# Hybrid GLA and Mamba-2 layer: conditioning weights in two column halves, raw first turns, an own bank for the turn of k

## The reference

```python
shift, scale, gate = jnp.split(jax.nn.silu(c) @ ada_w + ada_b, 3, axis=-1)
h    = rms_norm(x, pre_norm_w) * (1.0 + scale) + shift
proj = h @ w_in                       # q, k, v, g, gate code, z, xBC, dt
# GLA group, 4 heads, keys of 128, values of 256:
log_a = jax.nn.log_sigmoid(code @ gla_gate_w2 + gla_gate_b) / 16
o = rms_norm(gla_chunked(q, k, v, log_a), gla_norm_w) * jax.nn.silu(g)
# SSD group, 16 heads of 64: causal conv + SiLU on xBC, chunked scan, gated group norm -> y
mixed = jnp.concatenate([o, y], axis=-1) @ w_out
x = x + gate * rms_norm(mixed, post_norm_w)
```

## Time and profile before

| | |
|---|---|
| Time, median of 3 runs | 1843.85 us (1842.21 to 1844.53) |
| Profiled execution: its time | 1843.53 us |
| Profiled execution: its span | 1841.8 us |
| TensorE busy | 1692.6 us (92%), 9620 matmuls |
| VectorE, ScalarE, GpSimd busy | 879.9 (48%), 813.8 (44%), 241.6 us (13%) |
| DMA | 172.20 MB, mean 93 GB/s |
| Mean granted TensorE clock | 0.973 |

### The profile page before, as it was taken

How to read it: one execution, slowest core, us unless ns; L and a number is a source line. 1 busy time by engine, 2 the same in 40 slices (tenths; PEclk the granted TensorE clock), 3 DMA queues, 4 the chain that set the end, 5 groups by cost and what they waited for, 6 DMA issues and landing times. The chain is left out here.

```text
span 1841.8 us, 26172 instructions
## 1 busy us (share of the span) xinstructions
PE 1692.6 (92%) x9620; PEld 1456.8 (79%) x9620; DVE 879.9 (48%) x1593; ACT 813.8 (44%) x1412; POOL 241.6 (13%) x369
## 2 busy tenths in 40 slices
PE   2799989998999899988999999999999599999998
PEld 2578777777788778877889898888988477888886
DVE  5444443354343433345676668766676453222221
ACT  1565555545554555554445546545544441111110
POOL 5000000000000000000222121222222201000000
PEclk8799999999999999998999999999999899999999
DMA  8422151135122412224111134212210174222221
GB/s 255 144 87 104 50 169 58 53 113 156 62 62 72 119 61 67 80 58 126 64 64 63 63 109 144 75 64 68 91 57 34 58 239 150 91 91 91 91 91 46
DMA packets 102142, 172.20 MB, mean 93 GB/s; under 512 B 7459, under 2 KB 75315, under 8 KB 98086
## 3 DMA queue, kind: packets, MB, share of 16 engines
q1 hardware_dynamic: 98918, 154.05, 25.8%
q10 hardware_dynamic: 2304, 16.78, 2.4%
q0 software_dynamic: 832, 0.22, 0.1%
HBM read 137.21 MB, written 33.82 MB: 93 GB/s over the span
## 5 line engine op out<-in xcount | busy, mean ns | idle before, releaser
L960 PE MATMUL ps<-hl,w 128*128 128x512 f32 x1536 | 391.5, 405 | 0.0
L1841 PE MATMUL ps<-d_w,d_yh 128*128 128x512 f32 x1536 | 354.2, 393 | 16.6 <-DVE d_yh L1798 11.0
L1841 PEld LDWEIGHTS ps<-d_w,d_yh 128*128 128x128 f32 x1536 | 290.7, 190 | 80.0 <-DVE d_yh L1798 11.4
L960 PEld LDWEIGHTS ps<-hl,w 128*128 128x128 f32 x1536 | 288.4, 192 | 60.6 <-issue 0.9
L1577 PE MATMUL ps<-hl,w 128*128 128x256 f32 x2304 | 294.6, 288 | 5.1 <-POOL c_past L1266 5.1
L1577 PEld LDWEIGHTS ps<-hl,w 128*128 128x128 f32 x2304 | 282.5, 193 | 13.3 <-issue 7.7
L966 PE MATMUL ps<-w,hl 128*128 128x256 f32 x1536 | 201.1, 287 | 0.0
L966 PEld LDWEIGHTS ps<-w,hl 128*128 128x128 f32 x1536 | 191.3, 191 | 2.5
L1458 DVE SCALAR_TENSOR_TENSOR c_acc<-c_before,conv_col,c_acc 128x256 f32<-128x256 f32 x288 | 142.3, 494 | 79.8 <-ACT c_acc L1342 72.8
L1581 PE MATMUL ps<-hl 128*128 128x512 f32 x768 | 178.7, 392 | 0.0
L1581 PEld LDWEIGHTS ps<-hl 128*128 128x128 f32 x768 | 143.0, 188 | 29.4
(11 more groups left out here) (227 smaller groups left out, 2185.1 us busy)
## 6 DMA issues: line engine op xcount, KB each, us to landing
x_sb<-h SPq DMA_DIRECT2D x52, 512.0 KB, 3.9
c_ac<-step_sums ACTq DMA_DIRECT2D x16, 1024.0 KB, 4.7
w_raw<-in_w_in SPq DMA_DIRECT2D x30, 512.0 KB, 5.2
c_h_raw<-h SPq DMA_DIRECT2D x56, 256.0 KB, 2.8
d_y_raw<-mixed_in SPq DMA_DIRECT2D x7, 2048.0 KB, 8.6
ada<-in_ada_w SPq DMA_DIRECT2D x8, 1024.0 KB, 17.9
x_sb<-in_x SPq DMA_DIRECT2D x16, 512.0 KB, 6.7
mixed_in<-y SPq DMA_DIRECT2D x32, 256.0 KB, 2.5
```

The costliest lines, as they stand in the source:

```text
L960: mm = pe.matmul(ps[:, PROJ + u % 2, :], w[:, u, k, a, :], hl[:, par, k, b, :], start=(k == 0 and i == 0), stop=(k == KT - 1 and i == 2))
L1841: mm = pe.matmul(ps[:, 2 * t + j, :], yh[:, t, f, a, :], w[:, f, c, j * 512:(j + 1) * 512], start=(f == 0 and i == 0), stop=(f == FT - 1 a ...
```

## The change

Three things are changed, and the order of the first block's work follows from them.

- `ada` is held as two halves of the columns: shift and scale of columns 0 to 3 of tiles, then of 4 to 7. SP loads eight row blocks of the first half (0.5 MB each, pieces of 2 KB), block 0 of x, two weights, the eight row blocks of the second half, the third weight, block 1 of x. Each half is summed, multiplied into its own bank (`MODS`) and made into gains by itself.
- TensorE turns all of block 0 before it has any gain; ScalarE copies the raw turns to SBUF (`first_copy`), and scaling reads them there. Weights 0 and 1 are split next, and units 0 and 1 of step 0 are multiplied column by column beside the codes (`first_units`), columns 0 to 3 before, 4 to 7 after the second half's sum. Step 0 starts at slot 4. The squares and the norming of block 1 come before it, after the copies of units 0 and 1, of the code and the split of weight 3; the soft gate of step 0 moves from slots 2 and 3 to 4 and 5, `gate_sums` from 4 to 6, `exps` from 6 to 8, the splits of weights 4 and 5 to slots 5 and 7.
- The turn of k goes to bank `LEFT` in rounds 3, 5 and 7 to 14 (`k_turns`; round r is computed in step r+1), where it doesn't wait for y; the turn of o waits for y instead. In every step the table set with Exp and Ln is loaded right after Silu. In `ssd`, TensorE no longer waits for that block's constants at its start.

```diff
-    FIRST_TURNS = (2, 3, 4, 5, 7)
+    FIRST_TURNS = (2, 3, 4, 5)
+    MODS = (7, 5)
...
+        def k_turns(r):
+            return TURNS if r + 1 < NB or r + 1 in (SIZES_AT, GATE_AT + 1) else LEFT
...
-                def load_ada(k):
-                    sp.dma_start(ada[:, k, :], ada_w[0, k * P:(k + 1) * P, 0:2 * D]).then_inc(ada_loaded[k], 16)
+                def load_ada(j, r):
+                    wait(sp, ada_loaded[r], j * 16)
+                    src = ada_w[0, r * P:(r + 1) * P, 0:2 * D].rearrange("p (s n) -> p s n", s=2)
+                    sp.dma_start(ada[:, j, r, :].rearrange("p (s n) -> p s n", s=2), src[:, :, j * HK * P:(j + 1) * HK * P]
+                                 ).then_inc(ada_loaded[r], 16)
...
-                for k in range(KT):
-                    load_ada(k)
-                    if k == 1:
+                for r in range(KT):
+                    load_ada(0, r)
+                    if r == KT - 1:
                         load_x(0)
-                for u in range(AHEAD):
-                    load_w(0, u)
+                load_w(0, 0)
+                load_w(0, 1)
+                for r in range(KT):
+                    load_ada(1, r)
+                load_w(0, 2)
...
+                def first_copy(k):
+                    act.wait_ge(turned, k + 1)
+                    act.activation(first_full[:, k, :], ps[:, FIRST_TURNS[k % 4], :], ACT.Copy).then_inc(first_raw, 1)
...
                     act.activation(gz[:, n % 2], gz[:, n % 2], ACT.Silu).then_inc(gsilu, 1)
+                    act.preload_act_table_set("natural_log_exp_and_others")
...
+                    gate_at = 4 if n == 0 else 2
+                    for i in range(4 if n == 0 else 0, 3 * TB):
...
-                        if i == 2:
+                        if i == gate_at:
                             gate_in(n)
-                        if i == 3:
+                        if i == gate_at + 1:
                             soft_gate(n)
...
-                        if i % 2 == 1 and n == 0 and i // 2 + AHEAD < U:
-                            w_high(0, i // 2 + AHEAD)
+                        if n == 0 and i in (5, 7):
+                            w_high(0, (i - 5) // 2 + UV)
...
-                        if i == 6:
+                        if i == gate_at + 4:
...
-                act.wait_ge(gain_ready, 1)
+                for k in range(KT):
+                    first_copy(k)
+                w_high(0, 0)
+                w_high(0, 1)
                 for k in range(0, KT, 2):
-                    even_full(0, k, FIRST_TURNS[k % 5])
+                    act.wait_ge(gain_ready, k // HK + 1)
+                    if k == 0:
+                        act.wait_ge(first_raw, KT)
+                    even_full(0, k, first_full[:, k, :])
                     high(0, k)
                     high(0, k + 1)
-                    if k // 2 < AHEAD:
-                        w_high(0, k // 2)
+                    if k == HK - 2:
+                        w_high(0, 2)
+                code_part(0)
+                evacuate(0, 0)
+                evacuate(0, 1)
+                code_high(0)
+                w_high(0, 3)
+                for t in range(TB):
+                    x_square(1, t)
...
+                def add_ada(j, r):
+                    dve.wait_ge(ada_loaded[r], (j + 1) * 16)
+                    if r == 0:
+                        dve.tensor_scalar(ada_sum[:, j, :], ada[:, j, r, :], c_act[:, r:r + 1], None, ALU.mult
+                                          ).then_inc(sum_ready, 1)
+                    else:
+                        dve.wait_ge(sum_ready, j * KT + r)
+                        dve.scalar_tensor_tensor(out=ada_sum[:, j, :], in0=ada[:, j, r, :], scalar=c_act[:, r:r + 1],
+                                                 in1=ada_sum[:, j, :], op0=ALU.mult, op1=ALU.add).then_inc(sum_ready, 1)
+
+                def gains(j):
+                    ks = slice(j * HK, (j + 1) * HK)
+                    dve.wait_ge(mod_done, j + 1)
+                    dve.tensor_copy(mod[:, :, ks], ps[:, MODS[j], 0:KT].rearrange("p (s k) -> p s k", s=2)).then_inc(mod_ready, 1)
+                    dve.wait_ge(mod_ready, j + 1)
+                    dve.scalar_tensor_tensor(out=gain[:, ks], in0=mod[:, 1, ks], scalar=1.0, in1=pre_col[:, ks],
+                                             op0=ALU.add, op1=ALU.mult).then_inc(gain_ready, 1)
+                    dve.wait_ge(gain_ready, j + 1)
+
+                def first_pair(k):
+                    odd_full(0, k + 1, first_full[:, k + 1, :])
+                    low(0, k)
+                    low(0, k + 1)
+
                 dve.wait_ge(c_ready, 1)
-                for i, k in enumerate(BY_SUMS):
-                    dve.wait_ge(ada_loaded[k], 16)
-                    if i == 0:
-                        dve.tensor_scalar(ada_sum[:, :], ada[:, k, :], c_act[:, k:k + 1], None, ALU.mult).then_inc(sum_ready, 1)
-                    else:
-                        dve.wait_ge(sum_ready, i)
-                        dve.scalar_tensor_tensor(out=ada_sum[:, :], in0=ada[:, k, :], scalar=c_act[:, k:k + 1],
-                                                 in1=ada_sum[:, :], op0=ALU.mult, op1=ALU.add).then_inc(sum_ready, 1)
-                    if i == 1:
-                        x_normed(0)
+                for r in range(KT):
+                    add_ada(0, r)
                 dve.wait_ge(wg_hi, 1)
                 dve.tensor_tensor(wg[:, :, L0:L0 + RC], wg_raw[:, :, :], wg[:, :, 0:RC].bitcast(F32),
                                   ALU.subtract).then_inc(wg_ready, 1)
                 dve.wait_ge(w2_hi, 2)
                 dve.tensor_tensor(w2[L0:L0 + RANK, :], w2_raw[:, :], w2[0:RANK, :].bitcast(F32),
                                   ALU.subtract).then_inc(w2_ready, 1)
-                dve.wait_ge(mod_done, 1)
+                x_normed(0)
                 dve.wait_ge(cols_loaded, 32)
-                dve.tensor_copy(mod[:, :], ps[:, PROJ, 0:2 * KT]).then_inc(mod_ready, 1)
-                dve.wait_ge(mod_ready, 1)
-                dve.scalar_tensor_tensor(out=gain[:, :], in0=mod[:, KT:2 * KT], scalar=1.0, in1=pre_col[:, :],
-                                         op0=ALU.add, op1=ALU.mult).then_inc(gain_ready, 1)
-                dve.wait_ge(gain_ready, 1)
-                for k in range(0, KT, 2):
-                    odd_full(0, k + 1, FIRST_TURNS[(k + 1) % 5])
-                    low(0, k)
-                    low(0, k + 1)
-                    if k // 2 < AHEAD:
-                        w_low(0, k // 2)
+                gains(0)
+                dve.wait_ge(first_raw, KT)
+                first_pair(0)
+                w_low(0, 0)
+                w_low(0, 1)
+                for r in range(KT):
+                    add_ada(1, r)
+                    if r == 1:
+                        first_pair(2)
+                    if r == 3:
+                        w_low(0, 2)
+                gains(1)
+                first_pair(4)
+                first_pair(6)
+                code_sum(0)
+                code_low(0)
+                w_low(0, 3)
+                x_normed(1)
...
+                def mods(j):
+                    pe.wait_ge(sum_ready, (j + 1) * KT)
+                    bias = ada_col[:, :].rearrange("p (s k) -> p s k", s=2)[:, :, j * HK:(j + 1) * HK]
+                    pe.matmul(ps[:, MODS[j], 0:KT].rearrange("p (s k) -> p s k", s=2), ident[:, :], bias, start=True, stop=False)
+                    for f in range(KT):
+                        mm = pe.matmul(ps[:, MODS[j], f:f + 1], ada_sum[:, j, f * P:(f + 1) * P], ones[:, 0:1], start=False,
+                                       stop=(f == KT - 1))
+                    mm.then_inc(mod_done, 1)
+
+                def first_units(k):
+                    codes(0, k)
+                    for u in range(2):
+                        if k == 0:
+                            pe.wait_ge(w_ready, u + 1)
+                        for i, (a, b) in enumerate(PASSES):
+                            mm = pe.matmul(ps[:, PROJ + u, :], w[:, u, k, a, :], hl[:, 0, k, b, :],
+                                           start=(k == 0 and i == 0), stop=(k == KT - 1 and i == 2))
+                        if k == KT - 1:
+                            mm.then_inc(unit_done, 1)
...
                     wait(pe, kt_ready, m)
-                    wait(pe, y_ready, m)
+                    if k_turns(r) == TURNS:
+                        wait(pe, y_ready, m)
                     cols = slice(t * P, (t + 1) * P)
-                    pe.transpose(ps[:, TURNS, 0:DK], k_end[:, cols], ident[:, :]).then_inc(kt_done, 1)
+                    pe.transpose(ps[:, k_turns(r), 0:DK], k_end[:, cols], ident[:, :]).then_inc(kt_done, 1)
...
                     pe.wait_ge(kt_ready, m + 1)
+                    wait(pe, y_ready, m)
...
-                pe.matmul(ps[:, PROJ, 0:2 * KT], ident[:, :], ada_col[:, :], start=True, stop=False)
-                pe.wait_ge(c_ready, 1)
```

(49 more changed lines are left out.)

33 lines of the change are left out of this document (18 added, 15 removed).

## The result

| | before | after |
|---|---|---|
| time, median | 1843.03 us (1837.94 to 1844.53, 4 runs) | 1823.68 us (1822.90 to 1825.26, 4 runs) |
| ratio after/before, 95% interval | | 0.9901 (0.9880 to 0.9922) |
| profiled run / its span | 1843.53 / 1841.8 us | 1824.41 / 1822.7 us |
| ScalarE busy | 813.8 us | 783.7 us |
| granted clock, mean | 0.973 | 0.972 |

The account below looks back on a forecast made before the run. The prediction took TensorE's chain of waits, ending in an output projection fed without a break, as the bound. Terms of +8.3 and -27.0 net -18.7 us: a span of 1823.1, forecast 1825 us, range 1814 to 1838.

Parts of the forecast that it names:

- The opening: Up to the first turn of block 1: that turn at 87.2 us against 85.54, a loss of 1.7.
- Steps 0 to 2: Start of the gated attention: longer TensorE waits, +4.0 us in step 0 and +0.9 each in steps 1 and 2.
- the term of 0.8 for a low clock: In steps 0 to 2: longer gaps may buy one more low-clock stretch, +0.8 us (0 to 3).
- The table loads: Gated attention: three loads out, one in, per step; terms of -9.0, -6.3, -3.7, -1.5 and +1.8 us.
- The own bank: Gated attention: k's turn no longer waits for y in ten rounds; -5.1, -1.2 and -1.3 us.
- rival D: Table loads: the preload fails, Exp and Ln go on loading their own sets; 1843 us, no change; 6%.
- B: Opening: it gains after all, with x in by 19 and the clock high; 1816 us; 15%.
- C: Attention: waits are handed on to another input, so 27 saved becomes 14; 1838 us; 14%.
- E: Step 0 and three quarters of step 1: TensorE's clock stays low, costing 27 us more; 1852 us; 5%.
- The entry of the SSD part: Start of the SSD part: without the wait for constants TensorE starts at about 839.7, not 840.40; -0.7 us.

Follow-up runs that it names:

- e3_early_x: The changed kernel with the second block of x squared and normed ahead of the second half of the first units; 1812.12 us.
- e5_late_load: The changed kernel with the table load at the end of ScalarE's slot 7 instead of straight after Silu; 1813.22 us.
- e1_no_load: The changed kernel without the table load after Silu; 1831.87 us.
- e4_old_opening: The kernel before with the load, the bank and the entry of the SSD part changed, its opening left as it was; 1819.62 us.
- e8_bank_alone: The kernel before with the own bank for the turn of k as its only change; 1826.93 us.

## Why the prediction was right, point by point

**The opening** was worked out right in its order and nearly in its times. Last square at 23.76 (23.1 said), TensorE's turns from 31.40 (30.9), the second gain ready at 62.03 (63.1), block 1 at 86.52 (87.2). One size was off: the 32 turns took 5.56 us, 0.17 each, not 0.22. In the trace the first 18 start 0.21 us apart, the rate of the prediction, and the last 13 only 0.11. Half the distance looks like the clock's two levels, though the profile gives 1.00 for the whole stretch. The turns began 0.5 late and ended 1.1 early, and so the second half of the sums ended 1.2 early; the rest of the chain, a little longer than priced, left 0.7 of that. That block 1 waits because x is squared and normed behind the first units is shown by e3_early_x.

**Steps 0 to 2** cost 8.9 from block 1's turn to the start of step 3, where 6.6 was said. The waits are nearly those of the text: 2.87 at slot 6 of step 0 (3 said), 3.38 and 3.37 in steps 1 and 2 (3.4 said). At slot 8 of step 0 the 3.5 came in two pieces, 1.99 for the last weight, which the text had not named, and 1.37. What was too small is the term of 0.8 for a low clock: there were new stretches in steps 0, 2 and 3, and one in step 7 in place of another; only that of step 5 went.

**The table loads.** The mechanism was right: three loads out, one in, 1.28 each. The size was not. The sum had 15.6 us for the load alone; it is 9.5 in the kernel before and 8.2 in the changed one. The step that failed is the one that gave every step with a wait for o the full 2.55 and charged the added load with 0.9 in steps 3 and 7 alone: the last step of a head has the load in front of a weight split, which costs 1.0 of wait and 1.5 of clock there. With the load in its late place it brings what the sum said and more (e5_late_load is 18.7 below e1_no_load).

**The own bank** was under-priced, 7.6 against 15.4 alone and 11.4 in the changed kernel. Part of the gap is an account and not a size: five of the six waits for y behind o go with either part, as rival D has it, and the sum put them down to the load. Against D's 11.6 the bank alone is 3.8 better, and against 7.6 the bank in the changed kernel is 3.8 better too. The quiet steps 9, 10, 13 and 14 are shorter by 1.1 to 1.2 each, where 0.51 was said. Of that the bank alone gives 0.8 and the load alone 0.4. The part missed shows nowhere as a wait: before, at tile 2 of step 9, the turn of o takes 0.44 and in the kernel after 0.38, and the k behind it 0.30 against 0.27,

```profile
528.68 0.44 PE L1005 MATMUL ps<-ident,o_n 128*128 128x128 f32 x2
...
531.84 0.30 PE L979 MATMUL ps<-ident,k_end 128*128 128x128 f32 x1
```

```profile
525.75 0.38 PE L1076 MATMUL ps<-ident,o_n 128*128 128x128 f32 x2
...
528.74 0.27 PE L1049 MATMUL ps<-ident,k_end 128*128 128x128 f32 x1
```

and 0.44 and 0.30 are the lengths that the rows with a named wait have. The tile from 521.21 to 531.84 lasts 10.63 and that in the kernel after (518.56 to 528.74) 10.18. I read the 0.45 as stops too short to be listed; no run shows them by themselves.

**So the total was right partly by luck.** Taken alone, the load was priced 6.1 us too high and the bank 7.8 too low, and the two errors met in the sum. Set apart by e4_old_opening, the whole was closer than its parts: 23.1 outside the opening where the terms gave 23.9 (15.6 + 7.6 + 0.7), and 4.1 lost by the opening where they gave 5.2 (1.7 + 4.0 + 0.8, less 1.3 for the load in step 0). The range, 1814 to 1838, was wide enough for either error alone.

**The rivals.** B (the opening gains) and D (the preload does nothing) are out by the row at 86.52 and by the missing loads. C (waits handed on) is true of steps 3 and 7 and, with the load alone, of 11 and 15 (a wait of 2.26 in each), and false elsewhere. E (slower by the clock) had the right mechanism and far too large a size: the low stretches shown above cost 1.5 to 1.9 us each and end within their stages of 6 to 8 us.

**The entry of the SSD part** came 20.9 earlier and the end 19.1. The way from entry to end took 1001.4 before and 1003.2 after; over the other kernels it lies between 999.9 and 1004.0, also where nothing in it differs, so I read the 1.8 as scatter and not as a gain handed back. The wait of 5.15 is 4.31, 0.84 less, 0.7 said. It was not tried by itself.

## What to carry to other kernels

Price a wait of about 2 us or more on TensorE at its length plus the low clock that may follow it, here 1.5 to 1.9 us, and count an operation added ahead of such a wait the same way. Where an engine must do something once a step (here a table load), the place decides: 10 us lay between two places in the same slot. When work is split into halves so that one engine starts sooner, look at what the other engines now do behind it; and move a step forward only as far as its input is loaded.

## What the runs showed of the hardware

- A table load with an unrelated copy behind it costs 1.28 to 1.29 us in ScalarE's queue, no more (160.02 to 161.31).
- The granted clock of TensorE went from near 1.00 to 0.50 and back in these traces. In the attention's steps, over all kernels here, it was never low behind waits of TensorE under 1.9; behind waits of 1.94 to 2.89 sometimes (before, step 1 yes and step 2 no, and the other way round in e8_bank_alone, at the same wait of 2.4 to 2.5); behind those of 3.2 and more always.
- A transpose that has just been waited for is longer in the trace: 0.30 to 0.33 for a turn of k against 0.27, and 0.44 against 0.38 for the pair that turns o. Where one is longer without a listed wait, I take it as the sign of a stop too short to be listed, which is not shown.
